# Two-layer hybrid decoder step: page numbers, queries, routing weights and constants are placed elsewhere

## The reference

```python
s = (einsum('bqhr,bkr->bhqk', q_abs, c_kv) + einsum('bqhd,bkd->bhqk', q_rope, k_rope)) * scale
p = softmax(where(k_pos <= q_pos, s, -inf))
o = einsum('bhqk,bkr->bqhr', p, c_kv)             # c_kv: the request's pages, then its 8 new tokens
g_top, g_idx = top_k(softmax(xf @ w_grp + b_grp), 1)
e_top, e_idx = top_k(softmax(logits of the experts of group g_idx), 2)
weights = g_top * e_top / sum(e_top)              # one weight per token and choice
out = einsum('nef,ne,efd->nd', hid, combine, w_down)
```

## Time and profile before

| what | us |
|---|---|
| median of three runs | 2045.51 |
| the profiled execution | 2047.45 |
| its span, first to last instruction | 2045.7 |
| PE busy in it | 1795.5 (88%) |
| DVE, ACT, POOL busy | 752.7, 368.9, 75.2 |
| mean granted clock of PE | 0.936 of full speed |
| mean DMA rate | 220 GB/s |

### The profile page before, as it was taken

The page is one execution under the profiler, slowest core; times in us unless marked ns, Lnnn a source line. Parts: engine busy times, 40 slices in busy tenths (PEclk is TensorE's granted clock), DMA queues, the critical chain, the costliest instruction groups (busy, mean ns, idle before and its releaser), DMA issues. The chain is left out here.

```text
span 2045.7 us, 22901 instructions
## 1 busy us (share of the span) xinstructions
PE 1795.5 (88%) x8246; PEld 1071.1 (52%) x8246; DVE 752.7 (37%) x1569; ACT 368.9 (18%) x559; POOL 75.2 (4%) x73
## 2 busy tenths in 40 slices
PE   5999999979889978998579999998897899799884
PEld 2666667646446644432256666574573576443332
DVE  2152356646223342211135124565732242422113
ACT  1013112223102031111011312121420201311101
POOL 0000000000000001111000000000000000011110
PEclk7999998989999998999889999998998999799996
DMA  7565422323476847999555653224145677499992
GB/s 302 185 229 203 138 62 98 128 92 112 142 231 238 365 177 297 424 421 423 222 180 189 229 170 108 97 73 150 51 142 185 224 274 299 170 423 424 421 415 79
DMA packets 108571, 449.57 MB, mean 220 GB/s; under 512 B 19554, under 2 KB 54786, under 8 KB 80290
## 3 DMA queue, kind: packets, MB, share of 16 engines
q1 hardware_dynamic: 80882, 417.11, 54.2%
q10 hardware_dynamic: 18352, 20.39, 3.1%
q0 software_dynamic: 9216, 10.51, 1.5%
HBM read 442.17 MB, written 28.84 MB: 230 GB/s over the span
## 5 line engine op out<-in xcount | busy, mean ns | idle before, releaser
L371 PE MATMUL ps<-s_proj_and_h,w_in_tiles 128*128 128x320 f32 x1280 | 354.7, 438 | 16.8 <-DVE s_proj_and_h L234 16.8
L371 PEld LDWEIGHTS ps<-s_proj_and_h,w_in_tiles 128*128 128x128 f32 x1280 | 244.7, 193 | 131.1 <-issue 24.4
L186 PE MATMUL ps<-s_proj_and_h,w_in_tiles 128*128 128x320 f32 x960 | 293.4, 455 | 7.3 <-PEq L1191 6.0
L2104 PE MATMUL ps<-s_proj_and_h,t_ex_xf 128*64 128x512 f32 x1024 | 239.1, 622 | 30.1 <-DMA s_proj_and_h<-w_gate_up 28.4
L186 PEld LDWEIGHTS ps<-s_proj_and_h,w_in_tiles 128*128 128x128 f32 x960 | 186.0, 200 | 95.3 <-issue 34.4
L2104 PEld LDWEIGHTS ps<-s_proj_and_h,t_ex_xf 128*64 128x64 f32 x1024 | 81.3, 144 | 184.0 <-issue 184.0
L1785 PE MATMUL ps<-s_proj_and_h,w_merge 128*128 128x320 f32 x512 | 140.0, 437 | 3.8 <-PEq L1683 3.8
L1785 PEld LDWEIGHTS ps<-s_proj_and_h,w_merge 128*128 128x128 f32 x512 | 98.3, 192 | 45.6 <-issue 6.1
L2128 PE MATMUL ps<-w_down_slots,t_ex_hf 128*64 128x512 f32 x512 | 116.9, 599 | 2.5 <-DVE t_ex_hf L2175 1.0
L2173 DVE TENSOR_TENSOR t_ex_hid<-t_ex_hid,ps 128x256 f32<-128x256 f32 x32 | 13.5, 421 | 246.9 <-ACT t_ex_hid L2199 246.9
L1790 PE MATMUL ps<-s_proj_and_h,w_merge 128*128 128x320 f32 x256 | 71.3, 433 | 2.6 <-issue 2.6
(11 more groups left out here) (446 smaller groups left out, 2015.8 us busy)
## 6 DMA issues: line engine op xcount, KB each, us to landing
s_proj_and_h<-w_gate_up SPq DMA_DIRECT2D x64, 2048.0 KB, 22.5
w_in_tiles<-w_in SPq DMA_DIRECT2D x140, 512.0 KB, 3.6
w_down_slots<-w_down SPq DMA_DIRECT2D x64, 1024.0 KB, 22.7
w_mod_panels<-w_mod SPq DMA_DIRECT2D x32, 1024.0 KB, 7.6
page_keys<-pages_k SPq DMA_DIRECT2D x128, 192.0 KB, 3.3
w_merge<-w_branch SPq DMA_DIRECT2D x16, 1024.0 KB, 5.5
page_values<-pages_v ACTq DMA_DIRECT2D x96, 128.0 KB, 3.2
s_proj_and_h<-w_mod SPq DMA_DIRECT2D x8, 1024.0 KB, 16.5
```

Source lines behind the costliest of these rows:

```text
L186: mm = pe.matmul(K.ps[:, self.BANKS[i % 2], 0:T], self.win[:, j, k, :], K.h[:, k, :], start=(k == 0), stop=(k == KD - 1))
L371: mm = pe.matmul(K.ps[:, n % BANKS, 0:T], win[:, j, k, :], K.h[:, k, :], start=(k == 0), stop=(k == KD - 1))
L2104: mm = pe.matmul(K.ps[rows, GU, :], xf[:, k, rows], K.gate_up[:, j, k, :], start=(k == 0), stop=(k == KD - 1))
```

## The change

Page numbers: SP reads those of both halves of a pair before it waits for the first half. Queries: 4 copies instead of 24. Filler: four products ahead of the first scores, and five instead of six in each pair. Weights of the choices: the two exponentials and the arithmetic move from the router to the combine stage, and `rt_g` and `rt_st` outlive the router. Constants: only `ones`, `ident` and `eps` are loaded early, by ACT; all others follow the panels on SP's queue, and the wait for them moves to the projection stage of each layer. The rows of the product are copied by ACT and DVE, two each.

```diff
+            dve.wait_ge(K.consts_loaded, K.const_count)      # projection stage, ahead of small_done
+            act.wait_ge(K.consts_loaded, K.const_count)      # projection stage, ahead of dt_on_scalar
...
             for n in range(1, PAIRS):
+                pages = [page_numbers(K, sp, n, g) for g in range(2)]
                 for g in range(2):
-                    pages = page_numbers(K, sp, n, g)
                     sp.wait_ge(s("keys_used"), 2 * n - 1 + g)
-                    load_keys(K, sp, l, g, pages, A.keys)
+                    load_keys(K, sp, l, g, pages[g], A.keys)
...
+            F.products(pe, 4)
             pe.wait_ge(s("sa_q"), 1)
...
-                F.products(pe, 6)
+                F.products(pe, 5)
...
-            for b in range(NB):
-                for c in range(2):
-                    v.tensor_copy(qa_b[:, c, b]..., A.qa[:, c, :, SEQ + b * TS:SEQ + (b + 1) * TS])
-                ins = v.tensor_copy(qr_b[:, b // 4, b % 4]..., A.qr[:, :, SEQ + b * TS:SEQ + (b + 1) * TS])
+            for c in range(2):
+                v.tensor_copy(qa_b[:, c]..., A.qa[:, c, :, SEQ:T]...)
+                ins = v.tensor_copy(qr_b[:, c]..., A.qr[:, :, SEQ + c * NSAMP // 2:SEQ + (c + 1) * NSAMP // 2]...)
...
-            dve.wait_ge(s("rt_exp"), 1)                      # router; the next seven lines too
-            link(v.tensor_reduce(st[:, 5], g[:, 3], AX.X, ALU.add))
-            link(v.tensor_scalar(st[:, 6], st[:, 4], 1.0, None, ALU.add))
-            link(v.tensor_tensor(st[:, 6], st[:, 6], st[:, 5], ALU.mult))
-            link(v.reciprocal(st[:, 7], st[:, 6]))
-            link(v.tensor_tensor(st[:, 8], st[:, 7], st[:, 4], ALU.mult))
-            v.tensor_copy(R.w[:, 0], st[:, 7])
-            v.tensor_copy(R.w[:, 1], st[:, 8])
...
-            act.wait_ge(s("rt_garg"), 1)
-            nc.scalar.activation(g[:, 3], g[:, 2], ACT.Exp)
-            act.wait_ge(s("rt_darg"), 1)
-            nc.scalar.activation(st[:, 4], st[:, 3], ACT.Exp).then_inc(s("rt_exp"), 1)
...
+            dve.wait_ge(s("cb_exp"), 1)                      # combine, ahead of weigh(0); then the five
...
+            nc.scalar.activation(g[:, 3], g[:, 2], ACT.Exp)  # combine, behind ACT's three DMA issues
+            nc.scalar.activation(st[:, 4], st[:, 3], ACT.Exp).then_inc(s("cb_exp"), 1)
...
-            sp.wait_ge(once["consts_loaded"], 16 * (len(rest) + len(consts) - 1))
+            for name, dst in (("fin", K.fin), ("table", K.table), *((f"k_{n}", consts[n]) for n in consts if n not in first)):
+                sp.dma_start(whole(dst), d[name]).then_inc(K.consts_loaded, 16)
...
-            act.wait_ge(once["consts_loaded"], 16 * (len(rest) + len(consts) - 1))
+            act.wait_ge(once["rows_cleared"], 1)
+            act.wait_ge(once["mod_done"], 1)
+            for q in range(2):
+                ins = nc.scalar.copy(rows[32 * q:32 * q + NREQ, 0, :], K.ps[32 * q:32 * q + NREQ, 5, :])
+            ins.then_inc(once["mod_rows_copied"], 1)
+            act.wait_ge(once["eps_loaded"], 16)
+            nc.scalar.activation(spare[:, :], K.eps[:, 0:1], ACT.Sqrt)
...
-            dve.wait_ge(once["table_ready"], 1)
...
-            pe.wait_ge(once["consts_loaded"], 16 * (len(rest) + len(consts) - 1))
-            pe.wait_ge(once["mod_rows_copied"], 1)
+            pe.wait_ge(once["ident_loaded"], 16)
+            pe.wait_ge(once["mod_rows_copied"], 2)
```

More of the change, by code:

```diff
@@ L1632, in store_o @@
                 ins.then_inc(s("sa_o_copied"), 1)
-            for b in range(NB):
-                for c in range(2):
-                    v.tensor_copy(qa_b[:, c, b].rearrange("p (h t) -> p h t", t=TS), A.qa[:, c, :, SEQ + b * TS:SEQ + (b + 1) * TS])
-                ins = v.tensor_copy(qr_b[:, b // 4, b % 4].rearrange("p (h t) -> p h t", t=TS), A.qr[:, :, SEQ + b * TS:SEQ + (b + 1) * TS])
+            for c in range(2):
+                v.tensor_copy(qa_b[:, c].rearrange("p b (h t) -> p b h t", t=TS),
+                              A.qa[:, c, :, SEQ:T].rearrange("p h (b t) -> p b h t", t=TS))
+                ins = v.tensor_copy(qr_b[:, c].rearrange("p b (h t) -> p b h t", t=TS),
+                                    A.qr[:, :, SEQ + c * NSAMP // 2:SEQ + (c + 1) * NSAMP // 2].rearrange("p h (b t) -> p b h t", t=TS))
             link(ins)
@@ L1850, in router_stage @@
         bias = R.b_router
-        L, g = sb("rt_L", [P, 3, 36]), sb("rt_g", [P, 4, 3, 4])
-        ee, st, gate = sb("rt_e", [P, 5, 3, 8]), sb("rt_st", [P, 10, 3]), sb("rt_gate", [P, 3, 4, 8])
+        L, g, st = sb("rt_L", [P, 3, 36]), R.g, R.st
+        ee, gate = sb("rt_e", [P, 5, 3, 8]), sb("rt_gate", [P, 3, 4, 8])
         sel, tmp32 = sb("rt_sel", [P, 3, 3, NEXP]), sb("rt_tmp32", [P, 3, NEXP])
@@ L1923, in _ @@
             first_max(G, st[:, 0], g[:, 0], g[:, 1], 4)
-            v.tensor_tensor(g[:, 2], G, st[:, 0].unsqueeze(2).to_broadcast([P, 3, 4]), ALU.subtract).then_inc(s("rt_garg"), 1)
+            v.tensor_tensor(g[:, 2], G, st[:, 0].unsqueeze(2).to_broadcast([P, 3, 4]), ALU.subtract)
             link(v.tensor_tensor(gate[:, :, :, :], E, g[:, 0].unsqueeze(3).to_broadcast([P, 3, 4, 8]), ALU.mult))
@@ L1932, in _ @@
             first_max(ee[:, 2], st[:, 2], ee[:, 3], ee[:, 4], 8)
-            v.tensor_tensor(st[:, 3], st[:, 2], st[:, 1], ALU.subtract).then_inc(s("rt_darg"), 1)
+            v.tensor_tensor(st[:, 3], st[:, 2], st[:, 1], ALU.subtract)
             for n in range(2):
@@ L2212, in combine_stage @@
     yr = R.w_down[:, :, :, :].rearrange("p j a b -> p (j a b)")[:, 0:6 * D].rearrange("p (n r c) -> p n r c", n=2, r=3)
-    REG = ((0, P), (P, P), (SEQ, NSAMP))
+    REG, g, st = ((0, P), (P, P), (SEQ, NSAMP)), R.g, R.st
     def features(r):
@@ L2233, in weigh @@
                 dve.wait_ge(s(f"rows_loaded{r}"), 32)
-                link(v.tensor_scalar(yr[0:n, 0, r], yr[0:n, 0, r], R.w[0:n, 0, r:r + 1], None, ALU.mult))
-                v.scalar_tensor_tensor(out=yr[0:n, 0, r], in0=yr[0:n, 1, r], scalar=R.w[0:n, 1, r:r + 1], in1=yr[0:n, 0, r],
+                link(v.tensor_scalar(yr[0:n, 0, r], yr[0:n, 0, r], st[0:n, 7, r:r + 1], None, ALU.mult))
+                v.scalar_tensor_tensor(out=yr[0:n, 0, r], in0=yr[0:n, 1, r], scalar=st[0:n, 8, r:r + 1], in1=yr[0:n, 0, r],
                                        op0=ALU.mult, op1=ALU.add).then_inc(s("rows_summed"), 1)
@@ L2247, in onto_state @@
                 v.tensor_tensor(x, x, y, ALU.add).then_inc(s("x_ready"), 1)
+            dve.wait_ge(s("cb_exp"), 1)
+            link(v.tensor_reduce(st[:, 5], g[:, 3], AX.X, ALU.add))
+            link(v.tensor_scalar(st[:, 6], st[:, 4], 1.0, None, ALU.add))
+            link(v.tensor_tensor(st[:, 6], st[:, 6], st[:, 5], ALU.mult))
+            link(v.reciprocal(st[:, 7], st[:, 6]))
+            link(v.tensor_tensor(st[:, 8], st[:, 7], st[:, 4], ALU.mult))
             weigh(0)
@@ L2285, in begin @@
     panels = K.proj[:, :, :].rearrange("p n t -> p (n t)")[:, 0:KD * 2048].rearrange("p (k n) -> p k n", k=KD)
-    rest = ("fin", K.fin), ("table", K.table)
-    with nc.sbuf_tensor("bg_rows", [P, 1, 512], F32) as rows, nc.Block(no_gpsimd_drain=True) as block:
+    first = ("ones", "ident", "eps")
+    with (nc.sbuf_tensor("bg_rows", [P, 1, 512], F32) as rows, nc.sbuf_tensor("bg_spare", [P, 1], F32) as spare,
+          nc.Block(no_gpsimd_drain=True) as block):
         @block.sync
@@ L2293, in _ @@
                 sp.dma_start(panels[:, k], d["w_mod"][0, 0, k]).then_inc(once[f"panel_loaded{k}"], 16)
[L2294 to L2298, removed]
-            sp.wait_ge(once["consts_loaded"], 16 * (len(rest) + len(consts) - 1))
+            for name, dst in (("fin", K.fin), ("table", K.table), *((f"k_{n}", consts[n]) for n in consts if n not in first)):
+                sp.dma_start(whole(dst), d[name]).then_inc(K.consts_loaded, 16)
+            K.const_count = 16 * (2 + len(consts) - len(first))
         @block.gpsimd
@@ L2309, in _ @@
             act.dma_start(K.cols[:, :], d["cols"][0]).then_inc(once["cols_loaded"], 16)
-            for name in list(consts)[1::2]:
-                if name != "ones":
-                    act.dma_start(whole(consts[name]), d["k_" + name]).then_inc(once["consts_loaded"], 16)
+            for name in first[1:]:
+                act.dma_start(whole(consts[name]), d["k_" + name]).then_inc(once[name + "_loaded"], 16)
             act.wait_ge(once["c_loaded"], 16)
             nc.scalar.activation(K.silu_c[:, :, :], K.silu_c[:, :, :], ACT.Silu).then_inc(once["silu_c_ready"], 1)
-            act.wait_ge(once["consts_loaded"], 16 * (len(rest) + len(consts) - 1))
             act.wait_ge(once["silu_c_ready"], 1)
-            nc.scalar.activation(rows[:, 0, 0:1], K.eps[:, 0:1], ACT.Sqrt).then_inc(once["table_ready"], 1)
+            act.wait_ge(once["rows_cleared"], 1)
[5 more added lines that the diff above has]
+            nc.scalar.activation(spare[:, :], K.eps[:, 0:1], ACT.Sqrt)
         @block.vector
@@ L2323, in _ @@
```

(9 more changed lines are left out.)

3 lines of the change are left out of this document (2 added, 1 removed).

## The result

The changed kernel took 2055.47 us (median of six runs, 2050.72 to 2058.67), the kernel before 2045.55 beside it (six runs, 2042.09 to 2051.95): a ratio of 1.0049, with a 95% interval of 1.0027 to 1.007. The forecast was 2032.4, and 2041 the end of its range. The profiled execution has a span of 2056.5 us at a mean granted clock of 0.932, where the one before had 2045.7 at 0.936.

A forecast was written before the change was run, and what follows sets the result against it. PE, over 90% busy in nearly all slices, was taken as the bound, the experts as bound by transfers. Gains of 3.5 + 8.5 + 1.1 = 13.1 us from 2047.45, less 1.94 to the median, gave 2032.4 us; range 2023 to 2041.

The forecast's parts named there:

- Pairs two and three: Samples' attention, later pairs: keys asked for in one run beside the values cost 0.25 us per span, 1.0 in all (0 to 4).
- the run of keys starves the values: Attention: values served behind sixteen keys, plus PE's halved clock, lose 25.6 us over four spans; 2057 us, chance 0.07.
- Page numbers and queries: Attention's first later pair: keys' second half asked for earlier saves 9.5 us over both layers (5.5 to 12.2); queries add nothing.
- Start: Start of the kernel: earlier last panel and copies split between ACT and DVE save 3.5 us (2.1 to 4.2).
- Router: Router's end: DVE is free 2.6 us earlier, but the store of `h` limits the gather; 1.1 us saved in all (0 to 2.2).
- Combine: Combine stage: the moved exponentials and arithmetic hide behind DVE's wait for rows, costing nothing, with 1.3 us to spare.

The follow-up runs named there:

- x1: The changed kernel with SP again reading the page numbers of each half of the keys just ahead of that half; ratio 0.9958 to the kernel before.
- x2: The kernel before with only the page numbers of both halves read ahead of the first half of the keys; ratio 1.0023 to the kernel before.
- x4: The changed kernel with ACT asking for the second half of the values right behind the first, ahead of the exponential; ratio 0.9973 to the kernel before.
- z: x1 with all of `h` turned by PE and stored by ACT ahead of the late modulation's product; ratio 0.996 to the kernel before.
- x5: The changed kernel, SP holding the last two pairs' second half of keys until PE used the previous pair's first half of values; ratio 1.0005 to before.

## Why the prediction was wrong

- *Pairs two and three* is the step that failed: 0.25 us for each of four spans, 1.0 in all, bound 4. Measured 93.4 − 75.4 = 18.0, 4.5 a span. In the first layer's two later spans the values' later landing is 1.7 and 3.7 us of it, and the lower clock behind the wait 3.0 and 1.7. This step had no term for the clock. The prediction saw that the run of keys begins with the exponential, and took the 3.51 us of the earlier trace rows as a sign that keys beside values cost little. But there the second half of the keys came 1.7 us behind the exponential, and only five or so were asked for before the last value; in the first span after it were ten, in the second sixteen (worked out below). x1, x2 and x4 show this step by itself: the loss goes with the run, comes with it, and goes when the values are asked for first.
- The rival "the run of keys starves the values" is what happened: 4.5 us a span where it had 6.4, and past its point of decision, 3.5. Its parts were off (4.3 for the landing and 2.1 for the clock). That its 2057 us lie so near the measured 2055.5 is luck: its spans were 7.6 us too dear, its gains 2.4 too large (14.1 for 11.7), and 6 us lie elsewhere, unexplained. I gave it 0.07 because both queues move at once. That they do says nothing on who lands first.
- *Page numbers and queries*: 9.5 us forecast for the first pair; measured 4.5 in the first spans (41.9 to 37.4) and 4.2 between the first scores and the first exponentials, 8.7. Near as a sum, but by luck: its owner is wrong. The queries' part alone gives 8.1 in its own trace (its term was 0), because the first keys of the kernel before waited for the first scores and not for the numbers; beside it the numbers add nothing.
- *Start*: −3.5 forecast, −2.2 in this trace, near the lower bound; over nine traces −2.9, with the panel 0.7 us sooner where 1.4 was forecast.
- *Router*: −1.1 forecast, −0.8 measured, with the store as the next wait, 10.5 us to land. *Combine*: 0, the rows still release the product.

## What to carry to other kernels

Time that a queue spends on reading numbers can be what spaces its transfers: before closing such a gap, write down what the other queues ask for in it, and which of the two is needed first. A wait that was short at one phase says nothing of the same traffic shifted by a few us. And two parts that each shorten the same wait must be costed together and one by one, since the one can take the other's gain.

## What the runs showed of the hardware

- Two queues beside each other. Up to the last value's issue, 10 keys of 192 KB and 8 values of 128 KB (3.0 MB) were asked for from 563.08 on; at the 349 GB/s of that stretch they end at 571.7 (an estimate), 3.3 us before PE's 575.03. The same sum for before, with five keys, gives 575.7 and 579.10 (3.4), for the second collision, with sixteen, 594.8 and 599.15 (4.4). What each queue moved in the kernel after from 565.5 to 573.5 us stands in its DMA view (packets, MB, share of 16 engines; q1 has the keys, q10 the values):

```profile
q1 hardware_dynamic: 1113, 1.52, 55.3%
q10 hardware_dynamic: 1121, 1.02, 41.2%
```

  Both queues move packet for packet, but a packet of keys is larger, and the values get 40% of the bytes. In the second collision (589.5 to 597.5) it is 1144 and 1089 packets. The Trainium skill, "DMA: Bandwidth & Descriptors", section "Queues, rings and completion order", has engines take turns between queues; by that rule I let the rival fall. These counts agree with turns, and the values still landed too late: a share of 40% was not enough. Service in the order of issue would give the same counts here, since the requests alternate too, and in x1 from 562.5 to 563.5 the keys, asked for earlier, moved 219 packets and the values 30, though values had been asked for since 560.86. So which of the two rules holds stays open.
- The same 256 KB store took 2.9 us where `w_down` was asked for 2.0 us behind it (z), 9.2 to 10.5 where it had been asked for ahead of it (before, after, x1).
- After a stand of 3.51 us PE took 1.95 us for 16 instructions, at full clock; after 5.47 it took 3.68, at a granted clock of 0.50. The length of the stand alone doesn't decide it: twelve key instructions took 2.79 us at 1.00 behind a stand of 3.49 (after), and 4.35 us at 0.63 behind one of 2.68 (x5).
